# Cached keys scored inside the input projection, the recurrence moved to the value stage, all loads on one queue

## The reference

```python
mod = jnp.dot(jax.nn.silu(c), w_ada) + b_ada
sh1, sc1, gt1, sh2, sc2, gt2 = [m[:, None, :] for m in jnp.split(mod, 6, axis=-1)]
h = rmsnorm(x, g_pre1) * (1.0 + sc1) + sh1
proj = jnp.dot(h, w_in)
hq, hf, hi, hg, aq, ak, av, ua, ub = jnp.split(proj, splits, axis=-1)
f = lb + (1.0 - lb) * jax.nn.sigmoid(hf.astype(jnp.float32))
o_a, s_new = hgrn2_recurrence(hq, 1.0 - f, hi, jnp.log(f), s0, chunk)
o_a = rmsnorm(o_a, g_onorm) * jax.nn.silu(hg)
q, k, v = rope(aq, pos), rope(ak, pos), av
o_b = moba_attend(q, concat(k_past, k), concat(v_past, v), pos)
merged = jax.nn.sigmoid(ua) * jnp.dot(o_a, w_proj_a) + jax.nn.sigmoid(ub) * jnp.dot(o_b, w_proj_b)
x = x + gt1 * rmsnorm(jnp.dot(merged, w_out), g_post1)
h = rmsnorm(x, g_pre2) * (1.0 + sc2) + sh2
g_, u_ = jnp.split(jnp.dot(h, w_gu), 2, axis=-1)
x = x + gt2 * rmsnorm(jnp.dot(jax.nn.silu(g_) * u_, w_down), g_post2)
```

## Time and profile before

| | |
|---|---|
| runs, us | 769.69, 770.56, 771.26 |
| median, us | 770.56 |
| profiled execution, span, us | 767.2 |
| PE busy | 654.4 us (85%) |
| DVE busy | 409.3 us (53%) |
| ACT busy | 267.9 us (35%) |
| POOL busy | 86.0 us (11%) |
| memory read and written over the span | 219 GB/s |

### The profile page before, as it was taken

How to read it: one execution, slowest core, us unless ns; L and a number is a source line. 1 busy time by engine, 2 the same in 40 slices (tenths; PEclk the granted TensorE clock), 3 DMA queues, 4 the chain that set the end, 5 groups by cost and what they waited for, 6 DMA issues and landing times.

```text
span 767.2 us, 13224 instructions
## 1 busy us (share of the span) xinstructions
PE 654.4 (85%) x5195; PEld 549.4 (72%) x5195; DVE 409.3 (53%) x496; ACT 267.9 (35%) x382; POOL 86.0 (11%) x110
## 2 busy tenths in 40 slices
PE   4769999999945767758989689973999999999995
PEld 1268999899933656534524259962999999999993
DVE  0552322425579979964368435649435353543526
ACT  1244323533472212121121333433546464532412
POOL 2050000000053265001111100002100000000000
PEclk9979999999985998965597979996999999999997
DMA  8876887685457978987597998631165546445301
GB/s 329 310 287 220 296 309 272 247 304 193 152 195 226 307 278 292 343 274 255 194 345 266 381 339 275 207 111 55 58 185 153 174 145 187 150 152 182 96 1 62
DMA packets 94257, 168.93 MB, mean 220 GB/s; under 512 B 6449, under 2 KB 37865, under 8 KB 91010
## 3 DMA queue, kind: packets, MB, share of 16 engines
q1 hardware_dynamic: 76562, 137.68, 52.3%
q10 hardware_dynamic: 14368, 19.86, 7.8%
q0 software_dynamic: 3280, 10.71, 3.6%
HBM read 163.51 MB, written 4.72 MB: 219 GB/s over the span
## 4 chain that ended last, share of the span: by engine, by line
PE 70%; DVE 14%; DMA 4%; ACT 4%; issue 3%; POOL 2%; ACTq 1%; SPq 0%; DVEq 0%
PE ps L1248 18%; PE ps L1250 17%; PE ps L1249 17%; DVE KT L939 3%; PE ps L1396 3%; PE ps L1259 3%; PE ps L1458 2%; DMA ring<-w_in 2%; DMA ring<-cache_v 1%; PE ps L1427 1%; DMA ring<-w_ada 1%; DVE hx L1096 1%; PE ps L1377 1%; PE ps L1303 1%; PE ps L1590 1%
## 5 line engine op out<-in xcount | busy, mean ns | idle before, releaser
L814 DVE TENSOR_TENSOR w_lo<-ring,w_hi 128x1024 fp32r<-128x1024 f32 (+1 forms) x128 | 152.2, 1216 | 148.4 <-ACT w_hi L479 148.3
L1248 PE MATMUL ps<-h_hi,w_hi 128*128 128x288 f32 x704 | 211.8, 301 | 19.1 <-POOL h_lo L386 19.1
L1249 PE MATMUL ps<-h_lo,w_hi 128*128 128x288 f32 x704 | 209.3, 297 | 0.0
L1250 PE MATMUL ps<-h_hi,w_lo 128*128 128x288 f32 x704 | 208.5, 296 | 0.0
L479 ACT ACTIVATE w_hi<-ring 128x1024 fp32r<-128x1024 f32 (+1 forms) x128 | 129.9, 1043 | 164.1 <-PE ps L1250 92.9
L1248 PEld LDWEIGHTS ps<-h_hi,w_hi 128*128 128x128 f32 x704 | 133.6, 190 | 26.8 <-issue 13.4
L1250 PEld LDWEIGHTS ps<-h_hi,w_lo 128*128 128x128 f32 x704 | 134.1, 190 | 0.0
L1249 PEld LDWEIGHTS ps<-h_lo,w_hi 128*128 128x128 f32 x704 | 133.8, 190 | 0.1
L939 DVE STREAM_TRANSPOSE KT<-ring 128x2048 f32<-128x2048 f32 x32 | 72.0, 2280 | 1.8 <-PE ps L1377 1.8
L1377 PE MATMUL ps<-KT,Wk 128*32 128x128 f32 x1024 | 41.0, 315 | 31.7 <-DVE KT L939 31.7
L1377 PEld LDWEIGHTS ps<-KT,Wk 128*32 128x32 f32 x1024 | 32.1, 126 | 40.4 <-DVE KT L939 27.1
(11 more groups left out here) (285 smaller groups left out, 850.7 us busy)
## 6 DMA issues: line engine op xcount, KB each, us to landing
ring<-w_ada SPq DMA_DIRECT2D x24, 1024.0 KB, 6.9
ring<-cache_k SPq DMA_DIRECT2D x96, 256.0 KB, 4.0
ring<-w_in SPq DMA_DIRECT2D x22, 1024.0 KB, 10.2
ring<-w_gu SPq DMA_DIRECT2D x44, 512.0 KB, 4.7
ring<-cache_v SPq DMA_DIRECT2D x64, 256.0 KB, 6.4
ring<-w_down SPq DMA_DIRECT2D x10, 1024.0 KB, 5.0
ring<-cache_k ACTq DMA_DIRECT2D x32, 256.0 KB, 3.8
ring<-cache_v ACTq DMA_DIRECT2D x32, 256.0 KB, 5.5
```

The costliest lines, as they stand in the source:

```text
L814: dve.tensor_tensor(w_lo[:, par, k, :], slot4(s)[:, k, :], w_hi[:, par, k, :].bitcast(F32), ALU.subtract).then_inc(sem("lo_split"), 1)
L1248: pe.matmul(dst, h, x_hi, start=first, stop=False)
L1249: pe.matmul(dst, h, x_lo, start=False, stop=False)
L1250: return pe.matmul(dst, l, x_hi, start=False, stop=last)
```

## The change

One list, LOADS, now gives the order of everything that comes through the ring, and SP issues all of it, pages included; ACT and POOL issue no page any more. The groups of the projection are computed in a new order (GROUP): the attention's q, k and v first. ada(1) stands in two lots of four, before w2 and before w3; ada(2) moves to y1: three blocks between dense(26) and dense(27), three before dense(28), two after it.

From w8 on the projection and the keys are fused. For each of w8 to w20 PE computes a half of the block and then scores one or two key units, then the other half and again a unit or two (five units for two blocks); DVE forms a half of the next block's w_lo and then transposes those units; ACT copies in the same order. The beginning of the recurrence (sigmoid, logarithm, scan) is spread over w8 to w12 on ACT and DVE. Wk holds two sequences in turn, so that POOL waits before it builds the third.

The rest of the recurrence moves behind the projection: POOL starts diff(0) after w21, PE transposes for it and runs gram(0) and gram(1) during the gate, gram(2) to gram(7) after values 1, 3, 4, 6, 8 and 9, hgrn_states after value 10, hgrn_out after 11, the sample outputs after 12 to 15, the norm and states after 16, 17, 20 and 22. The steps of the prompt's attention follow each value from 19 to 28.

```diff
+    GROUP = (4, 5, 6, 1, 0, 2, 3, 7, 8, 9, 10)
+    FUSED = range(8, 21)
+    NKEY, NVAL = 4 * NSEQ, 4 * NSEQ
+
+    def units(w, half):
+
+        return [u for u in range(NKEY) if u * 2 * len(FUSED) // NKEY == 2 * (w - FUSED[0]) + half]
+
+    LOADS = [("ada", k) for k in range(8)] + [("w", 0), ("w", 1)] + [("ada", 8 + k) for k in range(4)] + [("w", 2)]
+    LOADS += [("ada", 12 + k) for k in range(4)] + [("w", w) for w in range(3, FUSED[0] + 1)]
+    for w in FUSED:
+        LOADS += [("w", w + 1)] + [("key", u) for u in units(w, 0) + units(w, 1)]
+    LOADS += [("val", v) for v in range(NVAL)] + [("w", w) for w in range(22, 27)] + [("ada", 16 + k) for k in range(3)] + [("w", 27)]
+    LOADS += [("ada", 19 + k) for k in range(3)] + [("w", 28)] + [("ada", 22), ("ada", 23), ("w", 29)]
+    LOADS += [("gu", w) for w in range(30, 52)] + [("w", w) for w in range(52, 64)]
...
+            def slot_free(n):
+
+                if n < NSLOT:
+                    return
+                kind, i = LOADS[n - NSLOT]
+                if kind == "ada":
+                    sp.wait_ge(sem("ada_used"), i + 1)
+                elif kind == "key":
+                    sp.wait_ge(sem("key_slots"), i + 1)
+                elif kind == "val":
+                    sp.wait_ge(sem("value_slots"), i + 1)
+                else:
+                    sp.wait_ge(sem("lo_split"), 2 * (i + 1))
...
+                if b >= 2:
+                    pool.wait_ge(sem("kt_used"), 4 * (b - 1))
...
+            pool.wait_ge(sem("w_used"), 2 * NW)
             pool.wait_ge(sem("b_ready"), 1)
             diff(0)
             diff(1)
...
+            for w in FUSED:
+                hi_w(w + 1)
+                if w == 8:
+                    act.wait_ge(sem("tile_out"), 16)
...
+                score_rows(w, 0)
+                if w % 2:
+                    if w == 15:
+                        act.wait_ge(sem("k_stored"), 32)
+                    evac_in(w // 2)
+                score_rows(w, 1)
+            scores(NSEQ - 1)
+            evac_in(10)
...
+            act.activation(hqt[:, :, :], hb[:, :, :], ACT.Exp).then_inc(sem("eb"), 1)
             level_exp(0)
...
+            level_exp(1)
             act.wait_ge(sem("shift_ready"), 1)
...
+            for li in range(2, 7):
+                level_exp(li)
...
+                    lo_half(w + 1, slot_of("w", w + 1), (w + 1) % 2, half)
+                    for u in units(w, half):
+                        turn_keys(u)
+                        if u % 4 == 0 and u >= 8:
+                            block_sums(u // 4 - 2)
...
+            dve.wait_ge(sem("w_used"), 2 * NW)
             for b in range(NSEQ):
                 if b + 2 < NSEQ:
                     choose(b + 2)
 
                 dve.wait_ge(sem("s_exp"), b + 1)
                 dve.transpose(Pt[:, b], S[:, b, :].rearrange("p (c n) -> p c n", n=32)).then_inc(sem("probs_ready"), 1)
+            dve.wait_ge(sem("eb"), 1)
+            dve.tensor_copy(stat[:, 328:332], hqt[:, :, TP - 1])
+            link(dve.tensor_copy(stat[:, 332:332 + HH * NSEQ].rearrange("p (h b) -> p h b", h=HH),
+                                 hqt[:, :, SAMP].rearrange("p h (b t) -> p h b t", t=TS)[:, :, :, TS - 1]))
+            dve.tensor_tensor(hqt[:, :, :], hqt[:, :, :], q, ALU.mult).then_inc(sem("qt_ready"), 1)
+            keep(0)
+            keep(1)
+            keep(2)
+            dve.wait_ge(sem("probs_sum"), 1)
+            link(dve.reciprocal(rden, ps[:, 1, 128:136]))
+            for j in range(4):
+                rows = slice(32 * j, 32 * j + 32)
+                ins = dve.tensor_copy(rrow[rows, :], rden[rows, :].rearrange("p (g j) -> p g j", j=4)[:, :, j])
+            ins.then_inc(sem("rden_ready"), 1)
+            for gi in range(3, 8):
+                keep(gi)
...
+            for w in range(2, 4):
+                for k in range(4 * (w - 2), 4 * (w - 2) + 4):
+                    ada(1, k)
+                for half in range(2):
+                    project(w, half)
+            turn_ada(1)
...
+                    if (w, half) == (FUSED[0], 0):
+                        pe.wait_ge(sem("v_tok"), 1)
+                    for u in units(w, half):
+                        cached_keys(u)
+                        if u % 4 == 2 and u >= 6:
+                            restrip(u // 4 - 1)
+            project(21, 0)
             restrip(NSEQ - 1)
-
-
+            project(21, 1)
+
+
+            pe.wait_ge(sem("own_out"), 1)
             pe.wait_ge(sem("gate_parts"), NSEQ)
-            pe.matmul(ps[:, 1, 0:64], fold, stat[:, 0:64], start=True, stop=True).then_inc(sem("gate_sum"), 1)
-            hgrn_out()
+            pe.matmul(ps[:, 7, 0:64], fold, stat[:, 0:64], start=True, stop=True).then_inc(sem("gate_sum"), 1)
+            pe.wait_ge(sem("tile_out"), 44)
+            pe.wait_ge(sem("kt_ready"), 1)
+            turn_hgrn(hkt, 2)
             pe.wait_ge(sem("row_max"), 1)
             pe.matmul(ps[:, 1, 64:72], fold[0:32, :], stat[0:32, 256:264], start=True, stop=True).then_inc(sem("max_spread"), 1)
-
-
-            after = {(0, 3): lambda: (probs_sum(), hgrn_sample_out(0)), (1, 0): lambda: hgrn_sample_out(1), (1, 1): lambda: hgrn_sample_out(2),
-                     (1, 2): lambda: hgrn_sample_out(3), (1, 3): lambda: sample_states(0), (2, 0): lambda: o_sum(),
-                     (2, 1): lambda: sample_states(1), (3, 1): lambda: sample_states(2), (4, 1): lambda: sample_states(3)}
+            turn_hgrn(proj[:, HI:HI + 4, :], 4)
+            gram(0)
+            gram(1)
...
+            for v in range(NVAL):
+                values(v)
+                if v in (1, 3, 4, 6, 8, 9):
+                    gram(2 + (1, 3, 4, 6, 8, 9).index(v))
+                if v == 3:
+                    probs_sum()
+                if v == 10:
+                    hgrn_states()
+                if v == 11:
+                    hgrn_out()
+                if 12 <= v < 16:
+                    hgrn_sample_out(v - 12)
+                if v == 16:
+                    o_sum()
+                    sample_states(0)
+                if v == 17:
+                    sample_states(1)
+                if v == 20:
+                    sample_states(2)
+                if v == 22:
+                    sample_states(3)
+                if 19 <= v < 19 + AH + 2:
+                    prompt_step(v - 19)
+                if v == 30:
+                    sample_out(0)
...
             dense(26, 0, m_hi, m_lo, 0, True, False, "y1_done")
             pe.wait_ge(sem("m_lo"), 2)
+            for k in range(3):
+                ada(2, k)
             dense(27, 1, m_hi, m_lo, 4, False, True, "y1_done")
+            for k in range(3, 6):
+                ada(2, k)
             dense(28, 0, m_hi, m_lo, 0, True, False, "y1_done", free=("y1_out", 0))
+            ada(2, 6)
+            ada(2, 7)
             pe.wait_ge(sem("y1_sq"), 1)
             sum_squares(y1sq, range(0, 4), 0, 7, 4, "y1_sum")
             dense(29, 1, m_hi, m_lo, 4, False, True, "y1_done")
+            turn_ada(2)
```

More of the change, by code:

```diff
@@ L1267, in turn_ada @@
                 for j in range(4):
[L1268 removed]
+                    ins = pe.transpose(ps[:, TURN_BANK[g], j * P:(j + 1) * P], arow[:, j * P:(j + 1) * P], ident)
                 ins.then_inc(sem("mod_rows_turned"), 1)
[L1271 to L1287 removed]
```

642 lines of the change are left out of this document (256 added, 386 removed).

## The result

The changed kernel takes 812.75 us (median of four runs, 811.48 to 815.5) against 770.91 in the same comparison: ratio 1.0552, 95% interval 1.0511 to 1.0593. 792.8 was forecast, with a range up to 812: the direction was right, but of 41.8 us of loss only 22 were forecast, and the time lies just above the range. The profiled execution has a span of 813.7, 46.5 more than before. Some executions of one and the same kernel take over 1.5% longer at a lower granted clock; the ratios and their intervals leave them out.

The account below looks back on a forecast made before the run. PE alone bounds the projection and DVE the key scoring, each idling under the other. Fused stage -43.7, value stage +51.6 and y1 +14.3 sum to +22.2, so 789.4 in span and 792.8 us in time, range 760 to 812.

Parts of the forecast that it names:

- Front: Input projection: PE stalls 4.8 before w2 and 4.7 before w3 for late weights, 11.8 us with the low clock.
- Fused stage: Projection fused with key scoring: six rounds of together about 141 us, gate sum at 290.7 instead of 334.44, -43.7.
- rival A: Projection fused with keys: rounds overlap, PE's sum holds, gate sum at 260; total -8.5, 762 us; chance 0.14.
- Gate: From the gate sum to gram(2): more work queued on ACT and DVE, gram(2) can start 25.4 us after it.
- Chain of grams: Value stage, gram(2) to end of gram(7): serial POOL, ACT, PE, DVE chain of 38.1 us, no longer hidden under keys.
- From gram(7) to the first prompt scores: Value stage after the grams: keep, states and copy 4.8, hgrn_out 4.9, then value 12, sample outputs and the rest 37.3.
- Prompt attention: First prompt scores to the next projection's first block: 62 us, not 66.2, pages having landed; bounds 46 and 66.2.
- y1: Stage y1, which takes ada(2): eight modulation blocks, a stall before w28 and mod_add(2) add 14.3 us; bounds 7.9 and 18.
- From the span to the time: Whole kernel: the median of runs lies 3.4 above the profiled span, so 789.4 becomes 792.8 us.
- B: Value stage keeps the full clock, values standing between grams: 158 instead of 172.6, total 778.5 us; chance 0.18.
- C: Fused rounds: gaps cost the clock, two of 1.1 in each of six rounds, 13 us more, 806; chance 0.16.
- D: Value stage: the recurrence hides behind the value loads, total -29.4, 741 us; chance 0.05.

Follow-up runs that it names:

- the first experiment: Changed kernel with w2 and w3 fetched ahead of the four modulation blocks before each, only load order changed; ratio 1.0319 to the kernel before.
- the fifth slot: Changed kernel with a fifth 1 MB ring slot taking the loads of w10, key unit 6, w13 and key unit 13; 801.2 us, ratio 1.0415.

## Why the prediction was half right

Each step of it went the way it said; those that cost were larger, the one that gained was smaller. Two steps failed in every trace of unchanged code: the length of a round in the fused stage, so that the gate sum came at 300.9 to 305.9 instead of 290.7, and the way from the gate sum to gram(2), 29.0 to 29.7 instead of 25.4. The misses behind gram(2) are mostly no larger than what traces of the same code differ by.

- **Front.** 4.8 and 4.7 of stall were forecast, 5.22 and 5.36 measured; the slot for w10 was free at 137.79, forecast 137. Right as far as the waits go, and the first experiment showed the place. What they cost was put at 11.8; without them the times fell by 16 to 18 and the trace by 6.5, so the price is open.
- **Fused stage.** Rounds of 25.6, 24.2, 22.9, 22.7 and 22.2 were forecast, 27.4, 26.2, 24.4, 24.5 and 23.7 came; with the end of the stage the gate sum is 10.2 late, and the gain 33.6 instead of 43.7. That PE's sum would not hold, against rival A, was right. The cause that I gave, a weight behind its predecessor in the slot, is neither shown nor refuted: the loads of w12 and w14 do start when the second half of the split before them ends (165.17 and 191.37), an edit that took this away by putting key units there made the rounds 28 to 32 us long, and the fifth slot, which took it away too, gained 11.5. The term that was mis-sized is the split of the round's second weight. The first weight's starts 6.3 to 8.2 after the slot is free, forecast 6.5. The second weight's was forecast to start at 15.2 (16.4 less its own 1.2) and starts 16.3 to 19.8 after it, 18.0 or more in five of the six rounds. I had followed the loads' landings and DVE's order by hand, but not ACT's queue, in which that weight's rounded copy stands behind the copies of PE's results. In the third round the slot is free at 191.40, ACT waits 6.50 for PE, makes its copies, and only then the rounded one, for which DVE has waited 6.19:

```profile
205.13 0.41 ACT L499 ACTIVATE proj<-ps 128x288 f32<-128x288 f32 x1 [6.50 <-PE ps L1191]
210.09 2.00 ACT L478 ACTIVATE w_hi<-ring 128x1024 fp32r<-128x1024 f32 x2
211.17 1.22 DVE L762 TENSOR_TENSOR w_lo<-ring,w_hi 128x1024 fp32r<-128x1024 f32 x1 [6.19 <-ACT w_hi L478]
```

That another order on ACT would give the missing 1.5 to 2 us a round back was not tried.

- **Gate.** gram(2) was forecast 25.4 after the gate sum and came 29.6 after it. The step that failed is the one that left the maxima where they were: DVE's operations with two inputs took longer beside POOL's products, 3.6 us up to the spread (four comparisons 2.7 of it, a product of 128 x 64 that took 1.22 instead of 0.22 another 1.0). The Trainium skill, page "SBUF — State Buffer", section "Who interferes with whom", says that a DVE instruction with two inputs in SBUF contends with a GpSimd instruction that reads SBUF and that a reduction does not; this case's trace agrees, 1.23 to 1.45 against 0.69 for the comparisons and 0.69 in both for the reduction. The prediction did not put the two engines side by side.
- **Chain of grams.** 38.1 forecast, 40.4 measured, 38.8 to 42.3 over eight kernels with the same chain. The mechanism, a serial chain that had been hidden under the keys and is now on the path, is shown by moving one member of it: 24.7.
- **From gram(7) to the first prompt scores.** 47 forecast (4.8 + 4.9 + 37.3), 50.3 measured. The term that was too small is the last, 42.7 measured, at a clock of 0.61 over the stretch; but the whole stretch took 44.3 to 50.6 in seven kernels with the same code, so the forecast lies inside. One row was misread: the 1.94 of the earlier trace rows is one value unit at the low clock, not two at the full one. It did not change the sum, since the ten values still fitted into the chain, but the bound of 46 for the next term was wrong by it.
- **Prompt attention.** 62 forecast, 64.2 measured (60.1 to 64.2 in the same kernels), at 0.66 where it had been 0.84: the pages were no longer waited for, as forecast, but PE was busy 53.92 us for 237 instructions where 309 had taken 53.95.
- **y1.** 14.3 forecast, 16.2 measured, 14 to 16 over eight kernels. The price was right, its inside not: I had put 5.5 on w28's place in the order, and another order gave nothing clear of the scatter, as the modulation blocks then waited instead.
- **From the span to the time.** 3.4 between a profiled execution and the median did not carry over: this one lies 1.0 above its median.

Of the rivals, B (full clock in the value stage) did not happen; of C's extra 13 us in the fused stage 10 came, at a granted clock of 0.92 there; how much of them is the clock, as C has it, and how much ACT's queue was not separated. A and D are out: the gate sum came at 300.88 and not 260, and the value stage cost 63.4 and not nothing.

## What to carry to other kernels

When work is moved out of the shadow of another stage, price the whole chain that it forms at its new place, with every engine that takes part, and ask which engines now work side by side that did not before. When loads share a ring, write down for each load which instruction frees its slot and how far ahead of its own use that instruction stands: where the two are neighbours on one engine, a whole landing is exposed, and a new order that only changes which load stands there moves the wait or makes it worse. Follow every engine's queue through such a loop, that of the copying engine too. The same move came out 0.8% ahead of the old kernel once the loads of the front were in another order, the ring had one more slot and the chain had its longest member on an engine with time to spare.

## What the runs showed of the hardware

- PE can be busy for 44.76 of 46 us and still get a clock of 0.58, in a stretch of values and four-column products. Over the whole way from gram(7) to the first prompt scores twelve dense products raised it from 0.61 to 0.90 in one kernel and from 0.74 to 0.82 in another. What decides between the two levels was not settled here.
- A two-operand DVE operation of 128 x 512 takes 0.69 with POOL idle and 1.23 to 1.45 beside POOL's products; a reduction of the same size takes 0.69 in both.
